# Opening of a decoder-trunk kernel: two loads move to ACT's queue, the norm weight rows are loaded only where they are read, the sample rows come in two transfers, and the first group is worked off in the order 1, 2, 3, 0

## What is computed

```python
u = rmsnorm(h, norm_mix[0])                    # h = x, tokens x 2048
u_ext = concat([last 15 normalised inputs (zeros for the prompt), u])
for g, w in enumerate((2, 4, 8, 16)):          # four groups of 512 columns
    pooled[g] = (sum of the last w rows of u_ext) / min(pos + 1, w)
d = pooled - u
h = h + (einsum('btgc,gcd->btgd', d, w_group) * scale)
h = h + square(relu(rmsnorm(h) @ w_up)) @ w_down
```

## Time and profile before

| | us |
|---|---|
| median of the three timed runs | 2444.81 |
| lowest, highest | 2442.03, 2445.05 |
| the profiled execution, its own time | 2444.91 |
| its span, first to last instruction | 2443.2 |
| PE busy | 2428.1 |
| DVE, ACT, GpSimd busy | 1154.1, 876.8, 472.8 |
| mean granted TensorE clock | 0.998 |

### The profile page before, as it was taken

The page is one execution under the profiler, slowest core; times in us unless marked ns, Lnnn a source line. Parts: engine busy times, 40 slices in busy tenths (PEclk is TensorE's granted clock), DMA queues, the critical chain, the costliest instruction groups (busy, mean ns, idle before and its releaser), DMA issues.

```text
span 2443.2 us, 43158 instructions
## 1 busy us (share of the span) xinstructions
PE 2428.1 (99%) x16326; PEld 2377.0 (97%) x16326; DVE 1154.1 (47%) x1325; ACT 876.8 (36%) x1048; POOL 472.8 (19%) x553
## 2 busy tenths in 40 slices
PE   9999999999999999999999999999999999999998
PEld 9999999999999999999887899999999999999997
DVE  6644444344444454543466775544444444434444
ACT  6333233233333333323344453333233233333332
POOL 7620022012101332210011112330022012101331
PEclk9999999999999999999999999999999999999999
DMA  6544454455445444555477764444454455445443
GB/s 235 172 151 153 147 149 153 146 149 152 146 150 150 146 150 140 149 142 152 157 260 239 235 194 153 148 146 152 149 147 152 148 147 153 147 149 152 147 148 116
DMA packets 198471, 389.03 MB, mean 159 GB/s; under 512 B 12277, under 2 KB 12533, under 8 KB 197929
## 3 DMA queue, kind: packets, MB, share of 16 engines
q1 hardware_dynamic: 197664, 385.78, 51.4%
q0 software_dynamic: 736, 2.27, 0.3%
HBM read 365.81 MB, written 22.65 MB: 159 GB/s over the span
## 4 chain that ended last, share of the span: by engine, by line
PE 97%; DMA 1%; DVE 1%; ACT 0%; issue 0%; SPq 0%; DVEq 0%; ACTq 0%
PE G L1574 30%; PE G L1575 30%; PE G L1576 30%; PE X L1859 1%; PE X L1810 1%; DMA gain<-in_mix_rows 1%; PE X L1852 1%; DMA w_raw<-in_pool_w 0%; PE G L1891 0%; PE G L1895 0%; PE G L1893 0%; PE X L1799 0%; PE X L1744 0%; DMA w_raw<-in_mlstm_w_in 0%; PE X L1789 0%
## 5 line engine op out<-in xcount | busy, mean ns | idle before, releaser
L1089 DVE TENSOR_TENSOR w_lo<-w_raw,w_hi 128x1024 fp32r<-128x1024 f32 x648 | 822.4, 1271 | 1181.5 <-ACT w_hi L774 1164.9
L774 ACT ACTIVATE w_hi<-w_raw 128x1024 fp32r<-128x1024 f32 x608 | 644.4, 1060 | 1305.5 <-PE G L1576 1276.3
L1574 PE MATMUL G<-op_hi,w_hi 128*128 128x320 f32 x2816 | 873.8, 310 | 0.0
L1576 PE MATMUL G<-op_hi,w_lo 128*128 128x320 f32 x2816 | 869.1, 309 | 0.0
L1575 PE MATMUL G<-op_lo,w_hi 128*128 128x320 f32 x2816 | 869.0, 309 | 0.0
L1574 PE MATMUL G<-a_hi,w_hi 128*128 128x320 f32 x2304 | 712.2, 309 | 1.7 <-DVE hT L1208 0.9
L1575 PE MATMUL G<-a_lo,w_hi 128*128 128x320 f32 x2304 | 711.3, 309 | 0.0
L1576 PE MATMUL G<-a_hi,w_lo 128*128 128x320 f32 x2304 | 711.3, 309 | 0.0
L1574 PEld LDWEIGHTS G<-op_hi,w_hi 128*128 128x128 f32 x2816 | 528.6, 188 | 3.6 <-issue 1.6
L1575 PEld LDWEIGHTS G<-op_lo,w_hi 128*128 128x128 f32 x2816 | 528.7, 188 | 2.6 <-issue 1.0
L1576 PEld LDWEIGHTS G<-op_hi,w_lo 128*128 128x128 f32 x2816 | 528.5, 188 | 0.0
(11 more groups left out here) (265 smaller groups left out, 876.0 us busy)
## 6 DMA issues: line engine op xcount, KB each, us to landing
w_raw<-in_ffn_w_up SPq DMA_DIRECT2D x256, 512.0 KB, 3.7
w_raw<-in_ffn_w_down SPq DMA_DIRECT2D x256, 512.0 KB, 3.7
w_raw<-in_mlstm_w_in SPq DMA_DIRECT2D x96, 512.0 KB, 3.8
w_raw<-in_mlstm_w_out SPq DMA_DIRECT2D x32, 512.0 KB, 4.0
cst<-in_state_mlstm_C SPq DMA_DIRECT2D x26, 512.0 KB, 4.6
out_C_sample<-cst SPq DMA_DIRECT2D x26, 512.0 KB, 3.3
w_raw<-in_pool_w SPq DMA_DIRECT2D x8, 512.0 KB, 11.0
w_raw<-in_state_mlstm_C SPq DMA_DIRECT2D x6, 512.0 KB, 4.0
```

The costliest lines, as they stand in the source:

```text
L774: act.activation(w_hi[:, c % RING], w_raw[:, c % RING], ACT.Copy).then_inc(w_hi_ok, 1)
L1089: v.tensor_tensor(w_lo[:, slot], w_raw[:, slot], w_hi[:, slot].bitcast(F32), ALU.subtract).then_inc(w_lo_ok, 1)
L1574: pe.matmul(G[:, m, 0:T], w_hi[:, slot, t, w], hi[:, k, :], start=first and t == 0, stop=False)
L1576: ins = pe.matmul(G[:, m, 0:T], w_lo[:, slot, t, w], hi[:, k, :], start=False, stop=last and t == CK - 1)
```

## The change

`vecs` and the first 512 columns of `gain` are issued by ACT, ahead of its first wait. Of `gain`, only rows 0 to 63 are loaded at first (128 KB and 384 KB in place of 256 KB and 768 KB); rows 96 to 127 (256 KB) are loaded by one more transfer, which SP issues behind the residual of group 3 and so ahead of pool chunk 4. The third part of `xrow` is loaded as rows 0 to 63 and rows 64 to 127; the sums of squares wait for the first, PE's sample matmuls for both. The tiles of group 0 are split by ACT in the order 1, 2, (chunk 0's `w_hi`), 3, 0, and by DVE in the order 1, 2, 3, (chunk 0's `w_lo`), 0, where before chunk 0's split stood behind tile 1 on both engines and the order behind it was 0, 2, 3. PE waits for all four tiles ahead of chunk 0, where it waited for two. `keep_warm` blocks have 10, 5, 3, 8 calls in place of 13, 5, 8, 6 (beside 9 at the very start).

```diff
-WARM = (13, 5, 8, 6)
+WARM = (10, 5, 3, 8)
+FIRST = (1, 2, 3, 0)
...
+        near_in = sem("near_in")
+        gain_end_in = sem("gain_end_in")
...
-            for t in range(TT):
-                src = A["x_prompt"][0, t * P:(t + 1) * P, :] if t < 2 else A["sample_rows"]
-                sp.dma_start(xrow[:, t, :], src).then_inc(x_in[t], 16)
-            sp.dma_start(gain[:, 0:NC], A["mix_rows"][:, 0:NC]).then_inc(gain_in[0], 16)
-            sp.dma_start(vecs[:, :], A["vec_cols"]).then_inc(vecs_in, 16)
+            for t in range(2):
+                sp.dma_start(xrow[:, t, :], A["x_prompt"][0, t * P:(t + 1) * P, :]).then_inc(x_in[t], 16)
+            sp.dma_start(xrow[0:NS, 2, :], A["sample_rows"][0:NS, :]).then_inc(x_in[2], 16)
+            sp.dma_start(xrow[NS:, 2, :], A["sample_rows"][NS:, :]).then_inc(near_in, 16)
             pool_load(0)
             pool_load(1)
             residual_load(0)
-            sp.dma_start(gain[:, NC:], A["mix_rows"][:, NC:]).then_inc(gain_in[1], 16)
+            sp.dma_start(gain[0:NS, NC:], A["mix_rows"][0:NS, NC:]).then_inc(gain_in[1], 16)
...
             residual_load(3)
+            sp.dma_start(gain[P - GP:, :], A["mix_rows"][P - GP:, :]).then_inc(gain_end_in, 16)
...
+            act.dma_start(vecs[:, :], A["vec_cols"]).then_inc(vecs_in, 16)
+            act.dma_start(gain[0:NS, 0:NC], A["mix_rows"][0:NS, 0:NC]).then_inc(gain_in[0], 16)
             act.wait_ge(consts, 1)
             act.activation(scol[:, 3:4], rcol[:, 3:4], ACT.Sqrt)
...
             d_hi(0, 1)
             tile_root(2)
+            d_hi(0, 2)
             split_pool(0)
-            for i in TURN[1:]:
-                d_hi(0, i)
+            d_hi(0, 3)
+            d_hi(0, 0)
             split_pool(1)
...
-            d_lo(0, 1)
+            for i in FIRST[:-1]:
+                d_lo(0, i)
             split_pool(0)
-            for i in TURN[1:]:
-                d_lo(0, i)
+            d_lo(0, 0)
             samples(1)
...
                         v.wait_ge(d_ok, KT)
+                        v.wait_ge(gain_end_in, 16)
...
             keep_warm(WARM[2])
             pe.wait_ge(x_in[2], 16)
+            pe.wait_ge(near_in, 16)
             pe.wait_ge(u_ok, 1)
             samples(0)
             keep_warm(WARM[3])
             for g in range(GROUPS):
                 for c in range(2):
                     n = 2 * g + c
-                    pe.wait_ge(d_lo_ok, MT * g + (4 if c else 2))
+                    pe.wait_ge(d_lo_ok, MT * g + (2 if g and c == 0 else 4))
```

More of the change, by code:

```diff
@@ L836, in d_hi @@
                 k = MT * g + i
-                n = (1, 2, 3, 0).index(i) if g == 0 else TURN.index(i)
+                n = (TURN if g else FIRST).index(i)
                 act.wait_ge(d_ok, MT * g + n + 1)
@@ L1159, in d_lo @@
             def d_lo(g, i):
-                k, n = MT * g + i, MT * g + TURN.index(i)
+                k, n = MT * g + i, MT * g + (TURN if g else FIRST).index(i)
                 v.wait_ge(d_hi_ok, n + 1)
```

## The result

The changed kernel is slower: 2452.21 us (median of 7 runs, 2450.14 to 2453.03) against 2444.34 us (7 runs, 2442.03 to 2445.05). The ratio is 1.0033, 95% interval 1.0023 to 1.0043, so 7.9 us or 0.3%. The prediction had 2444.4 us with a range that ended at 2446.4, and gave 0.03 to a loss of this size: it was wrong.

The account below looks back on a forecast made before the run. It took chunk 4's start, the later of a PE path (37.6 us) and a transfer path (37.36), to bound the kernel. Chunk 4 0.45 us earlier gave 2444.81 - 0.45 = 2444.4 us, range 2442.0 to 2446.4.

Parts of the forecast that it names:

- What bounds the kernel: Whole kernel: its end is set by chunk 4's start plus a constant; before, transfers were the later path by 0.90 us.
- PE path: Opening, up to chunk 4: chunk 0's start at 17.7 plus 19.88 us puts chunk 4 at 37.6 us.
- transfer path: Pool chunk 5's landing to chunk 4: -131, -393 and +262 KB, in sum -262 KB, 0.69 us earlier, chunk 4 at 37.36.
- Step 1: ACT ahead of its first wait: two issues of some 1.2 us, hidden by its 3.40 us wait for the first rows.
- Step 2: First input rows: 188 KB moving beside them delay the input and the DVE work on it by 0.47 us.
- Step 3: ACT's sample-row and vecs waits (0.22 and 0.94 us) go; 0.2 us reaches DVE, sample rows multiplied at 13.1.
- Step 4: Pool chunk 0 lands 0.33 us earlier, at 13.73; its w_hi is done at 14.79.
- Step 5: New tile order ahead of chunk 0: w_hi's end to chunk 0 grows from 2.1 to 2.95 us; chunk 0 at 17.7.
- Step 6: Behind chunk 0: samples(1) loses its 0.9 us wait for gain rows; costs and brings nothing.
- (c): Opening: slow small and 32-row transfers, first input 0.81 us late, chunk 4 at 38.1 to 38.4; 2445.0 us, chance 0.15.
- (b): At 12 to 21 us: idle time drops the clock to 1.2 GHz, price 1.71 us; 2446.0 us, chance 0.20.
- (a): Low clock stretch at 45.82 to 49.24 us goes away, 0.45 + 1.71 = 2.2 us less; 2442.6 us, chance 0.23.

Follow-up runs that it names:

- e1: Changed kernel with the sample rows in one transfer of 128 partitions again; 2446.27 us, 1.0011 against the kernel before.
- e2: Changed kernel with gain loaded for all 128 rows again, without the additional 32-row transfer; 2447.06 us, 1.0012 against the kernel before.
- e3: Kernel before with only the sample rows split into rows 0 to 63 and 64 to 127; 2445.40 us, 1.0006.
- e6: Kernel before with gain for 64 rows, and rows 96 to 127 issued ahead of pool chunk 4, all by SP; 2447.95 us, 1.0019.
- e4: Kernel before with the sample rows in two equal transfers split by columns; 2443.82 us, 1.0007.
- e8: Kernel before with the sample rows in two transfers, even and odd partitions; one run, 2444.05 us.
- e9: As e6, but the transfer of gain rows 96 to 127 issued last, behind pool chunk 7; 2444.64 us, 1.0003 against the kernel before.
- e12: e9 plus an unneeded transfer of the same 32 rows, at e6's place, spread over every fourth partition; 2446.29 us, 1.0008 against the kernel before.
- e5: Kernel before with vecs and the first gain columns (all rows) issued by ACT; 2444.91 us, 1.0007.
- e7: Kernel before with only the new order of group 0's tiles, the wait for all four and the keep_warm counts; 2443.34 us, 1.0002.
- e10: Kernel before with far and the residuals of groups 2 and 3 issued behind pool chunk 5; 2443.57 us, 0.9995.
- e11: Changed kernel with sample rows in one transfer and gain for all 128 rows; 2444.30 us, 1.0005 against the kernel before.

## Why the prediction was wrong, point by point

**What bounds the kernel: right.** Chunk 4 starts at the later of a PE path and a transfer path, and the end follows it. The experiments fit it: with a landing at 32.8 or later (after, e1, e2, e3, e6) a wait remained and chunk 4 followed the landing by 7.64 to 7.67 us; at 30.8 to 31.2 (before, e4, e8, e9, e12) by 7.2 to 7.3; and with an earlier landing or a later chunk 0 (e5, e7, e10) the wait went and PE's path decided. Only e11 has 0.3 us ahead of chunk 4 that neither path gives. There `w_lo` of chunk 4 took 1.71 us from 36.23 on (1.22 in e7 from the same time), so DVE's eviction began at 37.87 in place of 37.37: a third path, through DVE, that the two leave out.

**The transfer path: wrong in size and sign; this is the step that failed.** The prediction counted bytes at one rate: -262 KB, -0.69 us. Measured was +4.85 us. It had three terms. "-393 KB" and "-131 KB" bring nothing, since the 64 rows take as long as the 128 (e9). "+262 KB" at 0.69 us was 2.6 us (e6 against e9), beyond its bound of 1.08. And a term was missing: the sample rows' split was priced as an earlier semaphore and nothing else, and costs 2.0 us in the kernel before (e3) and 2.8 in the kernel after (e1). All three come from one omission: that the rate depends on which partitions a transfer writes.

The row that could have told it was on the table. The earlier trace rows has 242 GB/s at 22 to 24 us, where `far` is due, the only transfer of the opening that writes 64 partitions. e10 bears that out: with `far` and two residuals issued later, these 2 us run at 384, and 26 to 28 us at 272. I took it as a property of small transfers, and used it for the 32-row transfer only. The other slow row, 233 GB/s at 10 to 12 us, has another cause: no transfer with few partitions is due there, and with `vecs` and the first `gain` columns on ACT's queue (e5) these 2 us run at 399. What makes those two slow on SP's queue was not looked into. The Trainium skill, page SBUF — State Buffer, section Door 1: The DMA port swizzle (why `[64,N]` ≈ `[32,N]`), says it outright: a transfer's rate goes by how many of the 16 SBUF ports its partitions reach, and partitions 0 to 63 reach only half of them, the same half as 0 to 31, and 64 to 127 only the other half. The traces agree: 213, 185 and 190 GB/s for 64, 64 and 32 partitions beside 389. By that page e8's even partitions and e12's every fourth reach all ports, and they ran at 408 and 387. The rule that the prediction did cite, from the Trainium skill's page DMA: Bandwidth & Descriptors, section Rules for kernel authors, says that halves "serialize" and advises against them; I read it as no gain, not as a loss.

**Step 1, ACT's issues: right.** They stand at 0.81 to 1.81 us, and ACT still waits 2.77 us for the first rows.

```profile
0.81 0.42 ACTq L817 DMA_DIRECT2D vecs<-in_vec_cols  x1
1.27 0.54 ACTq L818 DMA_DIRECT2D gain<-in_mix_rows  x1
```

**Step 2, the inputs' delay: right for the first, wrong for the second.** The first square starts at 6.10, 0.39 us later (0.47 forecast). The second starts at 10.25 in place of 8.15, 2.10 us later. The runs split this in two: with ACT's two issues as changed but the sample rows in one transfer it starts at 9.37 (e1, 1.22 us later; 1.6 in e5, where ACT issues 256 KB of `gain` and not 128), and with the halves alone at 9.02 (e3, 0.87 later). "All of that moves by the same 0.47" was wrong. Why the second transfer suffers more than the bytes beside it, and from halves that are issued behind it, stays open.

**Step 3: right about `vecs`, wrong about the rest.** ACT does not wait for `vecs` any more, but its wait for the sample rows is 0.32 us in place of 0.22; the sample rows are multiplied at 14.98, not at 13.1, because of step 2 and the slow halves. **Step 4** falls with the transfer path: `w_hi` of chunk 0 starts at 16.27, not at 13.73.

**Step 5, the new order: right.** From `w_hi`'s end to chunk 0 are 2.78 us after (20.11 - 17.33), 3.10 in e7 (18.42 - 15.32), forecast 2.95, before 2.15. ACT and DVE in order of time, first ACT, after:

```profile
16.27 1.06 ACT L791 ACTIVATE w_hi<-w_raw 128x1024 fp32r<-128x1024 f32 x1 [0.95 <-DMA w_raw<-in_pool_w]
17.23 0.82 ACT L844 ACTIVATE a_hi<-X,vecs 128x256 fp32r<-128x256 f32 x2
...
17.72 0.48 DVE L1168 SCALAR_TENSOR_TENSOR a_lo<-X,vecs,a_hi 128x256 fp32r<-128x256 f32 x1 [1.15 <-ACT a_hi L844]
18.12 1.22 DVE L1095 TENSOR_TENSOR w_lo<-w_raw,w_hi 128x1024 fp32r<-128x1024 f32 x1
```

DVE stands still for 1.15 us ahead of tile 3 with `w_lo` of chunk 0 queued behind it, as the step said. The start of chunk 0 without the slow transfers is 18.54 (e11), against the forecast 17.7 and its bound of 18.2: the terms of the order hold, the missing 0.8 us are step 2's.

**Step 6: wrong.** `samples(1)` did not lose its wait of 0.9 us for the `gain` rows; it is 1.47 us now, since the 64 rows take the time of 128 and all ahead of them is late.

**The rivals.** (c), the bytes' gain does not come, was the right neighbourhood with a price of 0.1 to 0.4 us for what cost over 5. (b), the low clock in the opening, appeared in e7 and cost 0.1 us there; in the kernel after it came behind chunk 4's long wait and cost 1.2 us over before. (a) happened without its gain: in the kernel after, the clock is 1.00 over group 3's sample matmuls and what follows them (49 to 56 us), but the stretch behind the long wait took the place of this one. Where there is neither, in e1, e2 and e8 to e12, it shortens the way from chunk 4 to the norm sum by 1.3 us (36.85 against 38.15), not by the 1.71 that I took for it: part of it is taken back by a wait of 0.2 us ahead of chunk 6, and the rest I did not trace.

**The chances.** 0.06 were left for all that I did not see, beside four cases whose chances already added up to 1.00; the largest cost that I had bounded was 1.08 us for a transfer kind without a row of its own. Where a change makes a kind of transfer that the trace does not have, the bound belongs at a half or a quarter of the rate (262 KB in 2.6 us are 101 GB/s, a quarter of the 388).

## What to carry to other kernels

Price a transfer by the partitions it writes, not by its bytes alone: leaving out rows that are not read saves nothing if the rest lies in one half of the partitions, and cutting a full-width transfer into its upper and lower half about doubles its time (1049 KB took 2.0 to 2.8 us more); cut it by columns, or by even and odd partitions. A small transfer that is not urgent is not free when it stands ahead of an urgent one in a full queue: the 262 KB needed at 70 us delayed the chunk needed at 31 us by 2.6 us. And what is won ahead of a wait is lost in it: look for the second path to the same point (here the landing of pool chunk 5) before counting a gain.

## What the runs showed of the hardware

- Rate of a stretch in which such a transfer is due: on 64 neighbouring partitions 177 to 213 GB/s, on 32 177 to 219, on 64 even and odd ones 408, on 32 with a step of 4 387, on all 128 382 to 420, but 233 where `vecs` and the first `gain` columns are due. The share of busy transfer engines was 0.85 to 1.06 in all of them.
- The stretches at the 1.2 GHz level had different work before them: narrow matmuls without idle time before 45.82 in the kernel before (the same place in e3, e4, e5 and e7, but not in e8 to e12), 3.3 and 3.7 us of idle time in the kernel after and in e6, and 1.76 busy us of 3.35 in e7. e1, with 2.8 us of idle time at the same place as the kernel after, kept 1.00. What decides was not settled.
- Two small transfers on ACT's queue (319 KB) delayed the first input by 0.4 us and the second by 1.6 us, while pool chunk 5 landed no later (e5); with 188 KB there (e1) it was 0.6 and 1.2 us. It was not tried with one of them alone.
